# A two-layer transformer block in fp32: the moving tiles of 256 columns read in another order, and the split weights placed 64 bytes later

## The chip, the cores and the metric

One Trainium2 chip, one core of it. The metric is the device time of one execution in microseconds (us), the median of 3 runs. Smaller is better.

## What is computed

The input is one sequence of 256 tokens with 2048 features each, in fp32. The first layer normalises it, multiplies it with a wide input matrix, runs a latent attention of 16 heads and a gated convolution of width 3 side by side, projects both, mixes them with gates and projects once more. The second layer puts 16 meta tokens ahead of the 256, so that it works on 272, and again runs two branches: an attention over the 64 keys that an indexer selects, and a gated recurrence. What takes the time is the same everywhere, products with weights that are read once:

```python
h = _rmsnorm(x, pre_norm_g)
proj = jnp.einsum('bsd,de->bse', h, w_in)            # 2048 x 15424
...
q = jnp.einsum('bsr,re->bse', _rmsnorm(q_a, q_a_norm_g), w_q_b)
kv = jnp.einsum('bsr,re->bse', _rmsnorm(c_kv, kv_a_norm_g), w_kv_b)
y_mla = jnp.einsum('bse,ed->bsd', attn, w_o_mla)
y_conv = jnp.einsum('bse,ed->bsd', b_gate * conv * jax.nn.silu(z_conv), w_o_conv)
out = jnp.einsum('bsd,de->bse', merged, w_out)
...
proj = h @ w_in                                       # second layer, 2048 x 12368
p = jnp.einsum('btnc,ncd->btnd', y, w_branch)
x + merged @ w_out
```

## The kernel before

**Products in three terms.** A weight tile w and an operand tile x are each split into two fp32r numbers, w = w_hi + w_lo and x = x_hi + x_lo, and a product is the sum of three matmuls: w_hi with x_hi, w_hi with x_lo, w_lo with x_hi. All three add up in one PSUM bank.

**The tile.** In `tile` (line 1293 on) the weight, 128 rows by 128 columns, is the stationary operand, and the activation, stored with its 2048 features along 16 tiles of 128 partitions and its 256 tokens along the columns, is the moving one. So one matmul reads 128 stationary columns and 256 moving columns and writes 256 columns of a bank. Kinds that begin with "f" are of this form. Their moving operand has 256 columns (the constant `S`) in most phases; where the second layer needs the meta tokens too (operand `h2_all`) it has 272 (`T`). Kinds that begin with "t" have the roles turned: the activation is stationary and the weights move, 512 columns in the last phase (`wout2`) and two pieces of 128 in the value tiles of phase `kv`. Every matmul has a weight load of its own.

**The work list.** `plan_work` writes the whole program as a list of steps. The weights come in units of 1024 columns (512 KB): SP's queue loads a unit into one of 4 slots of `w_raw`, ACT rounds it into one of 3 slots of `w_hi` (line 1619), DVE subtracts to fill the same slot of `w_lo` (line 1927), and 24 matmuls of TensorE consume it. Units run two to three ahead of TensorE. Everything else (norms, rope, softmax, gates, the recurrence) is put between the units by `pump`.

**Where things lie.** `Memory.__init__` allocates tensors in SBUF one behind another. Per partition `w_raw` takes 16,384 bytes, `w_hi` and `w_lo` 12,288 bytes each. Behind them comes `hb`, which holds the operand tiles of the first layer as rows of 256 columns (1024 bytes), with 16 columns (`ODD`, 64 bytes) ahead of them and 16 behind. `ob_hi` and `ob_lo` hold rows of 272 + 16 columns (1152 bytes); where only the 256 tokens are wanted, the row is read from column 16 on. Counted in lines of 64 bytes from the start of `w_raw`, all split weight tiles begin on even lines, all moving tiles of 256 columns on odd lines, and the moving tiles of 272 columns on even lines.

Of the kernel before, what the change touches and what calls it, by code (L numbers as in the profile page):

```python
# [9 lines left out]
F32R = mybir.dt.float32r  # L10
# [6 lines left out]
P = 128  # L17
D = 2048
KT = D // P
S = 256  # L20
# [97 lines left out]
class Stream:  # L118
# [3 lines left out]
    def __init__(self, eng, own):  # L122
        self.eng, self.own, self.count, self.seen = eng, own, 0, {}
# [85 lines left out]
COLS = lambda m: slice(m * P, (m + 1) * P)  # L209
# [832 lines left out]
ODD = 16  # L1042
MAGIC = 1.5 * 2.0 ** 23
N_LVL = len(LEVELS) * P // 2
L0 = CONSTS["late"][0]

pair = lambda x: x.rearrange("p (h x) -> p h x", h=2)
four = lambda x: x.rearrange("p (a b) -> p a b", a=4)


class Memory:


    def __init__(self, nc, ctx, a):
        def sb(name, shape, dt=F32):
            return ctx.enter_context(nc.sbuf_tensor(name, shape, dt))

        self.raw = sb("w_raw", [P, N_RAW, UNIT])
        self.whi = sb("w_hi", [P, N_SPLIT, UNIT], F32R)
        self.wlo = sb("w_lo", [P, N_SPLIT, UNIT], F32R)  # L1060
        hb = sb("hb", [P, ODD + 2 * KT * S + ODD], F32R)[:, ODD:ODD + 2 * KT * S].rearrange("p (k n) -> p k n", k=2 * KT)
        self.hb_hi, self.hb_lo = hb[:, 0:KT, :], hb[:, KT:2 * KT, :]
        self.ob_hi, self.ob_lo = (sb(n, [P, KT, T + ODD], F32R)[:, :, 0:T] for n in ("ob_hi", "ob_lo"))
        self.arena = sb("arena", [P, 72 * 256])
        self.con = sb("con", [P, CONSTS["resident"][1]])
        self.cols = sb("cols", [P, P])
        self.rope1 = sb("rope1", [P, 2, S])
        self.fac = sb("factor", [P, 3, T])
        self.small = sb("small", [P, 256])
        self.scratch = [sb(f"scratch{i}", [P, T])[:, :] for i in range(5)]  # L1070
        self.heads = [sb(f"head_factor{i}", [P, T])[:, :] for i in range(3)]
        self.acc_a, self.acc_b = sb("acc_a", [P, S])[:, :], sb("acc_b", [P, S])[:, :]
        psum = [ctx.enter_context(nc.psum_tensor(f"bank{i}", [P, 512], F32))[:, :] for i in range(8)]
        self.proj, self.side = psum[:5], psum[5:]
        self.stats = [sb(f"stats{i}", [P, 8])[:, :] for i in range(6)]
        self.prob = [sb(f"prob{i}", [P, 416])[:, :] for i in range(2)]
        self.prob_t = [sb(f"probT{i}", [P, 384])[:, :] for i in range(2)]
        self.small2, small3 = sb("small2", [P, 64]), sb("small3", [P, 2 * HI])
        self.q_factor = sb("q_factor", [P, 2 * HA])
        self.best = sb("best", [P, 16])  # L1080

        r = self.region
        self.Q1, self.QR, self.K1 = r(0, 16, H1, S), r(16, 8, H1 // 2, S), r(24, 16, H1, S)
        self.V1, self.G1 = r(40, 16, 2, D), r(56, 16, KT, S)
        self.LAT = self.V1[:, 0, :].rearrange("p (k n) -> p k n", k=8)
        self.OUT1, self.GM, self.XR = r(40, 16, KT, S), self.K1, r(24, 16, KT, S)
        self.x_in, self.x_meta, self.xT = r(0, 16, 2, D), r(16, 8, D), self.G1
        self.rows_in, self.pos_i = r(24, 1, P), r(25, 1, S)[0:1, :].bitcast(I32)
        self.u_t, self.gate_t = r(56, 4, 4, S), r(60, 4, 4, S)
        self.kr1 = r(68, 1, S)  # L1090
        self.KR2, self.KI2 = r(64, 2, 2, S), r(48, 2.25, 2, T)
        self.pos_f, self.metaT = self.small[0:1, 0:S], self.small[:, :]
        self.metaf = self.metaT.rearrange("p (k n) -> p k n", k=KT)
        s2 = self.small2
        self.lb, self.oml, self.lbx, self.mx = s2[:, 0:8], s2[:, 8:16], s2[:, 16:32], s2[:, 32:40]
        self.acc_m, self.rkv_col, self.q_gain = s2[:, 40:56], s2[:, 56:58], s2[:, 58:59]
        self.wiT = small3[:, :]
        self.R, self.RR, self.RQ = self.fac[:, 0, 0:S], self.fac[:, 1, 0:S], self.fac[:, 2, 0:S]
        self.F2 = self.fac[:, 1, :]
        self.F2M = self.F2[:, NMETA:T]  # L1100

        self.QI, self.KI = r(0, 8, 8, S), r(8, 2, T)
        self.KA, self.QA, self.VA = r(9.25, 4.25, KVA, T), r(13.5, 8, HA, S), r(21.5, 6, 3, 512)
        self.FB, self.IB, self.QB = r(27.5, 8.5, HB, T), r(36, 12, 3, 1024), r(48, 8, HB, S)
        self.GA, self.GB = r(56, 16, KT, S), r(29, 16, KT, S)
        self.late = r(58, 6, CONSTS["late"][1] - L0)
        self.bias2, self.score2 = r(65, 2, 416), r(67, 2, 416)
        self.lvl, self.lvl_in = self.small[:, 0:N_LVL // 4].bitcast(U8), r(69, 2, N_LVL)
        self.prob_m = [self.rope1[:, i, :] for i in range(2)]
        self.Cb, self.Rb, self.kL, self.qL = r(0, 2, W2), r(2, 2, W2), r(4, 2, W2), r(6, 2, W2)  # L1110
        self.A, self.kK, self.kd, self.St, self.kM = r(8, 2, W2), r(10, 2, W2), r(12, 1, S), r(21.5, 2, W2), r(23.5, 4, 1024)
        self.xT2, self.OT = r(29, 16, KT, S), r(0, 16, 2, D)

        self.x_dram = nc.dram_tensor("x_kept", [P, KT * S], F32, kind="Internal").ap()
        self.x1_dram = nc.dram_tensor("x1_kept", [P, KT * S], F32, kind="Internal").ap()
        self.weights = {n: a[n] for n in ("w_in", "w_q_b", "w_kv_b", "w_o_conv", "w_o_mla", "w_out")}
        self.weights |= {"w_in_2": a["w_in_2"][0], "w_branch_a": a["w_branch_2"][0, 0],
                         "w_branch_b": a["w_branch_2"][0, 1], "w_out_2": a["w_out_2"][0]}
# [157 lines left out]
def tensor_engine(nc, m, plan, S_):  # L1276
# [6 lines left out]
    def mm(dst, lhsT, rhs, start=True, stop=True):  # L1283
        return nc.tensor.matmul(dst, lhsT, rhs, start=start, stop=stop, skip_group_check=True)  # L1284

    def operand_ready(name, k):
        if name in ("h2", "h2_all"):
            pe.wait_ge(*done["meta"])
            pe.wait_ge(*done["h2", k])
        elif name in ("lat_q", "lat_kv", "oc", "zm", "mg", "ya", "yb", "mg2", "h"):  # L1290
            pe.wait_ge(*done[name, k])

    def tile(s):
        i, t = s.args
        u, slot = plan.units[i], i % N_SPLIT
        hi_w = m.whi[:, slot, 0:u.size].rearrange("p (k n) -> p k n", k=u.nk)
        lo_w = m.wlo[:, slot, 0:u.size].rearrange("p (k n) -> p k n", k=u.nk)
        if t == 0:
            pe.wait_ge(*plan.split[i]["w_lo"])
        if u.k0 == 0:  # L1300
            pe.wait_ge(*s.of["bank"].after)
        dst = m.out_of(u, t, s.of["bank"].slot)
        kind, j = u.tiles[t][0], int(u.tiles[t][1])
        for k in range(u.nk):
            kt = u.k0 + k
            operand_ready(u.phase.operand, kt)
            x_hi, x_lo = m.operand(u.phase.operand, kt)
            first, last = kt == 0 and not (len(u.tiles) > 4 and t % 2), kt == u.phase.ktiles - 1
            if kind == "f":
                inst = mm(dst, hi_w[:, k, COLS(j)], x_hi, first, False)  # L1310
                inst = mm(dst, hi_w[:, k, COLS(j)], x_lo, False, False)
                inst = mm(dst, lo_w[:, k, COLS(j)], x_hi, False, last)
            else:
                w_hi, w_lo, to = hi_w[:, k, :], lo_w[:, k, :], dst
                if u.phase.name == "kv":
                    w_hi, w_lo, to = heads_kv(w_hi), heads_kv(w_lo), pair(dst)
                inst = mm(to, x_hi[:, COLS(j)], w_hi, first, False)
                inst = mm(to, x_lo[:, COLS(j)], w_hi, False, False)
                inst = mm(to, x_hi[:, COLS(j)], w_lo, False, last)
        if u.last:  # L1320
            inst.then_inc(S_("proj"), 1)
        elif t == len(u.tiles) - 1:
            inst.then_inc(S_("used"), 1)
# [261 lines left out]
    def x1_turn(s):  # L1585
# [5 lines left out]
        turn(b[:, P:S], m.xT2[:, k, P:S], ident).then_inc(S_("x1_t"), 1)  # L1591

    does = dict(tile=tile, constants=constants, warm=warm, pre_cols=pre_cols, x_tile=x_tile, row_sum=row_sum, row_spread=row_spread,
                cols=cols, angle=angle, meta_turn=meta_turn, rope=rope, scores1=scores1, turn1=turn1, mix1=mix1,
                ki_turn=ki_turn, qa_sum=qa_sum, tok_turn=tok_turn, index=index, scores2=scores2, turn2=turn2,
# [1017 lines left out]
```

## Time and profile before

| | |
|---|---|
| median of 3 runs | 1958.9 us (1958.53 to 1958.91) |
| the profiled execution, its own time | 1948.82 us |
| its span (first to last instruction) | 1947.5 us |
| TensorE matmul (PE) busy | 1933.1 us, 99%, 15806 matmuls |
| TensorE weight load (PEld) busy | 1899.4 us, 98%, 15806 loads |
| DVE / ACT / POOL busy | 60% / 45% / 16% |
| DMA | 343.79 MB, mean 177 GB/s |
| granted TensorE clock, mean | 0.998 of full |

The profile names an instruction by engine, line, operation, and "out<-in" by tensor names; `bank<-hb,w_hi` is a matmul that writes a PSUM bank, with `hb` as moving and `w_hi` as stationary operand. Matmuls overlap each other in the records: one is listed with about 280 ns though the next begins far sooner, so the busy time of PE tells nothing of its speed. What tells it is the distance from one start to the next. The timeline gives the starts (neighbours of the same kind are merged there, with xN behind them), and the view by stretches gives how many matmuls lie in a stretch.

### The profile page before, as it was taken

What the parts mean: (1) busy time and instruction counts of PE and PEld (TensorE: products, weight loads), DVE (VectorE), ACT (ScalarE), POOL (GpSimd) and SP (SyncE); (2) the same over time, 40 slices, a digit from 0 to 9 for tenths busy, and PEclk for the clock granted to TensorE, in tenths of its full rate; (3) what the DMA queues carried; (4) which work ended last, traced back from release to release, by engine and by line L of the source; (5) the groups of instructions that cost most, each with busy time, mean ns of one, the idle gap of its engine ahead of it and who ended that gap; (6) DMA issues with size and microseconds to landing.
All of it is one profiled execution on the core that took longest, in us unless ns stands there. A gap on an engine that the chain in (4) does not pass through costs nothing.

```text
span 1947.5 us, 37136 instructions
## 1 busy us (share of the span) xinstructions
PE 1933.1 (99%) x15806; PEld 1899.4 (98%) x15806; DVE 1174.3 (60%) x1708; ACT 880.8 (45%) x1265; POOL 314.9 (16%) x320
## 2 busy tenths in 40 slices
PE   8999999999999999999999999999999999999999
PEld 8999999999999999999999999999999999999987
DVE  7765665556555455654664665676467776654644
ACT  6444454544444434444445543445443333444443
POOL 3210010202010002300122252040011132110200
PEclk9999999999999999999999999999999999999999
DMA  7565555566666566566565564544564444666564
GB/s 262 155 193 173 164 150 152 166 181 184 186 187 198 189 190 179 183 197 195 192 228 189 179 217 130 143 140 122 161 184 142 133 140 142 174 200 188 185 231 157
DMA packets 175919, 343.79 MB, mean 177 GB/s; under 512 B 10494, under 2 KB 19578, under 8 KB 175226
## 3 DMA queue, kind: packets, MB, share of 16 engines
q1 hardware_dynamic: 174106, 337.16, 57.3%
q10 hardware_dynamic: 1648, 4.26, 0.6%
q8 instruction: 124, 2.03, 0.4%
q14 instruction: 41, 0.34, 0.0%
HBM read 335.09 MB, written 6.29 MB: 175 GB/s over the span
## 4 chain that ended last, share of the span: by engine, by line
PE 94%; DVE 1%; issue 0%; POOL 0%; ACT 0%; POOLq 0%; ACTq 0%; DVEq 0%
PE bank L1284 93%; DVE w_lo L1927 1%; DVE hb L2163 0%; ACT w_hi L1619 0%; DVE scratch L2033 0%; DVE ob_lo L2138 0%; POOL scratch L2523 0%; PE bank L1501 0%; PE bank L1590 0%; PE bank L1440 0%; PE bank L1441 0%; PE bank L1439 0%; PE bank L1591 0%; PE bank L1503 0%; POOL acc_a L2452 0%
## 5 line engine op out<-in xcount | busy, mean ns | idle before, releaser
L1927 DVE TENSOR_TENSOR w_lo<-w_raw,w_hi 128x1024 fp32r<-128x1024 f32 (+2 forms) x644 | 785.9, 1224 | 484.8 <-ACT w_hi L1619 483.3
L1619 ACT ACTIVATE w_hi<-w_raw 128x1024 fp32r<-128x1024 f32 (+2 forms) x644 | 662.9, 1032 | 891.7 <-PE bank L1284 882.9
L1284 PE MATMUL bank<-hb,w_hi 128*128 128x256 f32 x4896 | 865.1, 280 | 1.7 <-DVE hb L1951 1.4
L1284 PEld LDWEIGHTS bank<-hb,w_hi 128*128 128x128 f32 x4896 | 745.9, 188 | 5.0 <-DVE w_lo L1927 3.5
L1284 PE MATMUL bank<-hb,w_lo 128*128 128x256 f32 x2448 | 681.7, 278 | 0.0
L1284 PE MATMUL bank<-ob_hi,w_hi 128*128 128x256 f32 (+1 forms) x2224 | 640.4, 288 | 0.1
L1284 PE MATMUL bank<-ob_lo,w_hi 128*128 128x256 f32 (+1 forms) x2224 | 624.8, 281 | 0.0
L1284 PE MATMUL bank<-ob_hi,w_lo 128*128 128x256 f32 (+1 forms) x2224 | 624.2, 281 | 0.0
L1284 PEld LDWEIGHTS bank<-hb,w_lo 128*128 128x128 f32 x2448 | 459.8, 188 | 0.0
L1284 PEld LDWEIGHTS bank<-ob_hi,w_hi 128*128 128x128 f32 x2224 | 418.1, 188 | 2.5 <-DVE w_lo L1927 0.5
L1284 PEld LDWEIGHTS bank<-ob_lo,w_hi 128*128 128x128 f32 x2224 | 418.1, 188 | 1.6
L1284 PEld LDWEIGHTS bank<-ob_hi,w_lo 128*128 128x128 f32 x2224 | 417.4, 188 | 0.0
L1284 PE MATMUL bank<-arena 128*128 128x64 f32 (+4 forms) x618 | 101.7, 302 | 2.6 <-ACT arena L1844 1.6
L1284 PEld LDWEIGHTS bank<-arena 128*128 128x128 f32 x618 | 80.9, 191 | 4.9 <-ACT arena L1844 2.3
L2533 POOL TENSOR_TENSOR arena<-scratch,arena 128x256 f32<-128x256 f32 x32 | 38.4, 1230 | 266.6 <-DVE scratch L2033 266.6
L2033 DVE TENSOR_TENSOR scratch<-bank,factor 128x256 f32<-128x256 f32 (+1 forms) x132 | 52.7, 421 | 36.4 <-PE bank L1284 36.3
L1284 PE MATMUL bank<-w_hi,ob_hi 128*128 128x512 f32 (+1 forms) x192 | 68.9, 359 | 0.0
L1284 PE MATMUL bank<-w_lo,ob_hi 128*128 128x512 f32 (+1 forms) x192 | 68.4, 356 | 0.0
L1284 PE MATMUL bank<-w_hi,ob_lo 128*128 128x512 f32 (+1 forms) x192 | 68.1, 354 | 0.0
L2506 POOL TENSOR_TENSOR arena<-arena,factor 128x256 f32<-128x256 f32 x16 | 19.2, 1233 | 269.3 <-DVE arena L2033 269.3
L2523 POOL TENSOR_TENSOR scratch<-scratch,head_factor 128x256 f32<-128x256 f32 x16 | 12.6, 787 | 236.1 <-ACT head_factor L1737 236.1
L2033 DVE TENSOR_TENSOR arena<-bank,factor 128x256 f32<-128x256 f32 (+1 forms) x86 | 34.4, 419 | 23.6 <-PE bank L1284 23.6
(241 smaller groups left out, 1171.4 us busy)
## 6 DMA issues: line engine op xcount, KB each, us to landing
w_raw<-in_w_in SPq DMA_DIRECT2D x436, 512.0 KB, 3.7
w_raw<-in_w_out SPq DMA_DIRECT2D x64, 512.0 KB, 4.4
w_raw<-in_w_o_conv SPq DMA_DIRECT2D x32, 512.0 KB, 4.1
w_raw<-in_w_o_mla SPq DMA_DIRECT2D x32, 512.0 KB, 4.0
w_raw<-in_w_branch SPq DMA_DIRECT2D x32, 512.0 KB, 4.1
w_raw<-in_w_kv_b SPq DMA_DIRECT2D x16, 512.0 KB, 3.7
w_raw<-in_w_q_b SPq DMA_DIRECT2D x16, 384.0 KB, 3.3
arena<-x_kept SPq DMA_DIRECT2D x2, 2048.0 KB, 9.4
```

The costliest lines, as they stand in the source:

```text
L1284: return nc.tensor.matmul(dst, lhsT, rhs, start=start, stop=stop, skip_group_check=True)
L1619: act(dst, src, ACT.Copy).then_inc(S_("w_hi"), 1)
L1927: tt(low, src, high.bitcast(F32), ALU.subtract).then_inc(S_("w_lo"), 1)
L2033: tt(dst, m.proj[s.of["pb"]][:, 0:dst.shape[1]], factor, ALU.mult).then_inc(S_("evac"), 1)
L2506: tt(m.u_t[:, t, :], m.u_t[:, t, :], m.R, ALU.mult).then_inc(S_("conv_b"), 1)
L2523: tt(z, z, ring[s.of["head"].slot][:, 0:S], ALU.mult).then_inc(S_("silu"), 1)
L2533: tt(y, m.scratch[s.of["scratch"].slot][:, 0:S], y, ALU.add).then_inc(S_("merged"), 1)
```

## The change

It changes two things and nothing else. The number of instructions on each engine and their order stay as they are.

1. Each "f" matmul whose moving tile has 256 columns reads it, and writes its 256 output columns, in another order: in runs of 16 columns (64 bytes), taking run 0, then 8, then 1, then 9, and so on to 7 and 15. Every column still gets the same sum at the same place. Moving tiles of 272 and 512 columns and the value tiles of `kv` keep their order.
2. A tensor of 16 columns (64 bytes) that nothing uses is allocated between `w_raw` and `w_hi`, and the 16 columns ahead of the operand tiles in `hb` go away. So `w_hi` and `w_lo` begin 64 bytes later, and all that comes behind keeps its place. Counted as above, all split weight tiles now begin on odd lines.

```diff
+twos = lambda x: x.rearrange("p (b a e) -> p a b e", b=2, e=16) if x.shape[1] == S else x
...
         self.raw = sb("w_raw", [P, N_RAW, UNIT])
+        sb("odd", [P, ODD])
         self.whi = sb("w_hi", [P, N_SPLIT, UNIT], F32R)
         self.wlo = sb("w_lo", [P, N_SPLIT, UNIT], F32R)
-        hb = sb("hb", [P, ODD + 2 * KT * S + ODD], F32R)[:, ODD:ODD + 2 * KT * S].rearrange("p (k n) -> p k n", k=2 * KT)
+        hb = sb("hb", [P, 2 * KT * S + ODD], F32R)[:, 0:2 * KT * S].rearrange("p (k n) -> p k n", k=2 * KT)
...
             if kind == "f":
-                inst = mm(dst, hi_w[:, k, COLS(j)], x_hi, first, False)
-                inst = mm(dst, hi_w[:, k, COLS(j)], x_lo, False, False)
-                inst = mm(dst, lo_w[:, k, COLS(j)], x_hi, False, last)
+                x_hi, x_lo, to = twos(x_hi), twos(x_lo), twos(dst)
+                inst = mm(to, hi_w[:, k, COLS(j)], x_hi, first, False)
+                inst = mm(to, hi_w[:, k, COLS(j)], x_lo, False, False)
+                inst = mm(to, lo_w[:, k, COLS(j)], x_hi, False, last)
```

## Rows read from the trace of the kernel before

**Rows 1.** The page: the span, and the chain that ended last by engine.
```profile
span 1947.5 us, 37136 instructions
...
PE 94%; DVE 1%; issue 0%; POOL 0%; ACT 0%; POOLq 0%; ACTq 0%; DVEq 0%
```

**Rows 2.** Groups of PE by form: count, busy us, mean ns | idle before.
```profile
L1284 PE MATMUL bank<-hb,w_hi 128*128 128x256 f32 x4896 | 865.1, 280 | 1.7 <-DVE hb L1951 1.4 <-DVE w_lo L1927 0.2
L1284 PE MATMUL bank<-hb,w_lo 128*128 128x256 f32 x2448 | 681.7, 278 | 0.0
L1284 PE MATMUL bank<-ob_hi,w_hi 128*128 128x256 f32 x1824 | 518.7, 284 | 0.1
...
L1284 PE MATMUL bank<-ob_hi,w_hi 128*128 128x272 f32 x400 | 121.6, 304 | 0.0
```

**Rows 3.** PE by stretches: from:to, us, busy (matmuls), granted clock, DMA share, GB/s.
```profile
410.00:560.00 150.00, 149.99 (x1274) 1.00 0.63 183
580.00:640.00 60.00, 60.00 (x532) 1.00 0.66 194
660.00:730.00 70.00, 70.00 (x602) 1.00 0.59 188
750.00:830.00 80.00, 79.97 (x676) 1.00 0.60 181
850.00:910.00 60.00, 60.00 (x532) 1.00 0.67 200
930.00:1000.00 70.00, 70.00 (x602) 1.00 0.58 189
```

**Rows 4.** PE timeline near 500 us: start us, listed us, instruction, how many.
```profile
500.13 0.40 PE L1284 MATMUL bank<-hb,w_hi 128*128 128x256 f32 x2
...
501.19 0.28 PE L1284 MATMUL bank<-hb,w_hi 128*128 128x256 f32 x1
```

**Rows 5.** PE timeline near 600 us.
```profile
600.02 0.39 PE L1284 MATMUL bank<-hb,w_hi 128*128 128x256 f32 x2
...
600.70 0.28 PE L1284 MATMUL bank<-hb,w_hi 128*128 128x256 f32 x1
```

**Rows 6.** PEld timeline near 500 us: the weight loads beside rows 4.
```profile
500.02 0.31 PEld L1284 LDWEIGHTS bank<-hb,w_hi 128*128 128x128 f32 x2
500.25 0.19 PEld L1284 LDWEIGHTS bank<-hb,w_lo 128*128 128x128 f32 x1
```

**Rows 7.** PE timeline near 1862 us: last phase, and four transposes in it.
```profile
1862.17 0.39 PE L1284 MATMUL bank<-w_hi,ob_hi 128*128 128x512 f32 x1
...
1865.18 0.39 PE L1284 MATMUL bank<-w_hi,ob_lo 128*128 128x512 f32 x1
...
1865.65 0.27 PE L1590 MATMUL bank<-con,arena 128*128 128x128 f32 x1
...
1865.98 0.27 PE L1591 MATMUL bank<-con,arena 128*128 128x128 f32 x1
```

**Rows 8.** PE timeline near 1160 us: moving tiles of 272 columns.
```profile
1159.98 0.29 PE L1284 MATMUL bank<-ob_hi,w_hi 128*128 128x272 f32 x1
...
1161.11 0.29 PE L1284 MATMUL bank<-ob_hi,w_hi 128*128 128x272 f32 x1
```

**Rows 9.** PE timeline near 140 us: value tiles of phase kv, moving in two pieces.
```profile
140.52 0.28 PE L1284 MATMUL bank<-w_hi,ob_hi 128*128 128x256 f32 x1
...
141.10 0.28 PE L1284 MATMUL bank<-w_lo,ob_hi 128*128 128x256 f32 x1
```

**Rows 10.** Waits: who waited for whom: us in total, times, longest.
```profile
PEld bank L1284 <- DVE w_lo L1927: 4.1, 11, 1.6
...
ACT w_hi L1619 <- PE bank L1284: 882.9, 527, 3.6
```

**Rows 11.** The page: the split of a unit on DVE, and the load of one.
```profile
L1927 DVE TENSOR_TENSOR w_lo<-w_raw,w_hi 128x1024 fp32r<-128x1024 f32 (+2 forms) x644 | 785.9, 1224 | 484.8 <-ACT w_hi L1619 483.3
...
w_raw<-in_w_in SPq DMA_DIRECT2D x436, 512.0 KB, 3.7
```

## The prediction

> **What bounds the kernel now.** First the chain of waits, summed by engine: TensorE holds 94% of the span [rows 1], and of its weight loads' waits the longest sum is 4.1 us, for `w_lo` [rows 10]. ACT, on the other hand, waited 882.9 us for TensorE to give weight slots back [rows 10]. So the work that feeds TensorE has room, and the time is the number of matmuls times the distance between two starts. The groups by form give the numbers: with a moving tile of 256 columns there are 4896 + 2448 from `hb`, and 1824 in each of three groups from `ob`, 12,816 in all; the tiles of 272 columns are 3 x 400 [rows 2].
>
> Then the distance, the number on which all hangs. By stretches: six stretches hold 490 us and 4218 matmuls; a matmul is listed for 0.28 us, so each stretch also counts some 2.4 that began before it, and 490 us over 4204 is **116.6 ns** [rows 3]. It isn't one pace: 1274 in 150 us is 118.0 ns and 532 in 60 us is 113.3 ns [rows 3]. The timelines say the same: from 500.13 to 501.19 lie nine starts, 117.8 ns each [rows 4], from 600.02 to 600.70 six, 113.3 ns each [rows 5]. The instructions, the tensors (`hb`, `w_hi`, `w_lo`) and the granted clock (1.00, the level of 2.4 GHz) are alike. At that clock 256 columns, one in each cycle, are 106.7 ns. So 7 to 11 ns of each matmul are lost to something that depends on how two things fall together in time, not on what is computed.
>
> What falls together? The next weight load begins within 10 ns behind each matmul's start (500.25, beside the second of the two that are merged from 500.13 on) [rows 4, 6]. Stationary and moving columns are read from the same memory side by side. And what a pair can't go below is seen in the transposes of the last phase, 128 moving columns and a weight load each: three distances in 0.33 us, 110 ns [rows 7], though 128 columns in one pass are 53 ns. I take **110 ns** as the floor of a load and matmul pair.
>
> **The change, part by part.**
>
> *The order of the columns.* It adds and removes no instruction. In the order before, moving lines of 64 bytes alternate between odd and even every 16 columns, 6.7 ns; the stationary lines alternate every 13.8 ns (110 ns over 8 lines). If memory has two sides, chosen by odd and even lines, then the two streams must meet on one side for half the time, wherever they begin. In the new order two lines of the same side follow each other, 0 and 8, then 1 and 9, so both streams change sides every 13 to 14 ns: once they are apart they stay apart. That such sides exist no row shows directly; what speaks for it is that the loss grows with the moving columns and isn't a fixed cost per matmul: 272 columns take 125.6 ns (nine distances in 1.13 us) against 113.3 at the clock [rows 8], 512 columns take 231.5 ns (13 in 3.01 us) against 213.3 [rows 7]; and that two paces exist at all. The cost is bounded from both sides. Below: the floor of 110, or 106.7 if the weight load could go faster than in transposes; above: load and read strictly one after the other, 110 + 107 = 217 ns. The old order, which meets half the time, pays only 6.6 ns over the floor, so I take the value near the lower end: 116.6 - 110 = 6.6 ns, times 12,816: **-85 us**.
>
> A rule speaks against this. The Trainium skill (SBUF — State Buffer, "Who interferes with whom") says that TensorE has two independent read ports, one for the moving operand and one for the weights, and never waits on anyone; by that rule the sum of this part would be 0. Rows 4 and 5, two paces of the same instructions, are hard to square with it, but they don't name the memory as the cause.
>
> *Reading and writing in runs.* A read in pieces is seen once: the value tiles of `kv` move two pieces of 128 columns and take 116 ns (five distances in 0.58 us) [rows 9], no more than their neighbours. For runs of 16 and for output in runs there is no row; I put them at 0 (the read row is the nearest), with the rival below as the upper end.
>
> *The weights 64 bytes later.* ACT and DVE write them at another address, in operations of the same length (DVE 1224 ns a unit [rows 11], against 24 x 116.6 = 2800 ns that TensorE needs for it). What changes is with which line both streams begin: before, stationary even and moving odd; now both odd. Whether that is the right side can't be read from the trace, since the two reads' true offset isn't in it. In my forecast it costs 0; the wrong side is a rival. For the tiles of 272 columns the order stays and only this shift acts: at most the difference of the two paces, 4.5 ns, up or down, times 1200, +-5 us; I take 0.
>
> *What is late next.* At 110 ns a unit lasts 24 x 110 = 2640 ns. The load of a unit lands in 3.7 us with up to four in flight, and the DMA share of 0.57 to 0.67 [rows 3] becomes at most 0.67 x 117/110 = 0.71. DVE's split still fits, but other DVE work stands in the same queue, so some more waits for `w_lo` come: I double the 4.1 us [rows 10], **+4 us**.
>
> Sum: -85 + 4 = **-81 us**. Against the profiled execution, 1948.8 us, that is 1868; the median of the runs is 1958.9, 10 us above it, and the same difference gives **1878 us**.
>
> **The rivals.**
>
> 1. *Only the better of the two present paces.* The streams settle at 113.3 ns everywhere, as in rows 5. For it: that pace is held for 60 us on end twice [rows 3], so it is a stable state. Against it: it arises with the old order. (116.6 - 113.3) x 12,816 = 42 us: 1917 us.
> 2. *Nothing changes* (the change does not do what its order suggests). The loss is inside TensorE or on the way of each column, and order and place of the lines don't matter. For it: the loss per column is nearly the same for 256, 272 and 512 columns, though in the last case the weight load ought to be over after half the time. 1959 us, within the +-5 us of the other tiles.
> 3. *Slower: both streams begin on the same side.* The new order keeps two moving lines on one side, so a wrong start costs a whole stationary line, 13.8 ns, before they are apart, and every matmul with its own weight load begins anew: 110 + 13.8 = 123.8 ns, 7.2 ns more than now, times 12,816: +92 us, 2051 us. It decides from the point where more than 6.6 ns of each start are lost, half a line. For it: both operands now begin on odd lines and within 10 ns of each other [rows 6]. Against it: the loads' data may be wanted a line earlier or later than the starts say, in which case the shift is just what sets them apart. A smaller loss is as possible as a whole line.
> 4. *Slower: the output in runs.* 16 runs a matmul instead of one; if each of the 15 jumps costs one cycle, 0.42 ns, the gain of 6.6 ns is used up (6.3), and with two cycles each matmul takes 110 + 12.5 = 122.5 ns: +76 us, 2035 us. No row has such an output. The Trainium skill (PSUM — Partial Sum Buffer, "Specifications") says that PSUM has lines of 8 bytes and any non-contiguous pattern slows matmuls significantly. By that rule this is the case; no run here shows it, and within a run of 16 columns everything is contiguous, so I hold it less likely.
>
> **How the numbers follow.** Forecast 0.48, rival 1 0.17, rival 2 0.09, rival 3 0.16, rival 4 0.10. Differences under 0.2% (4 us) can't be told from no change here. Faster by more: 0.48 + 0.17 = 0.65. Within: 0.09. Slower: 0.26. The forecast's own range is 1850 (108 ns a pair, as the floor is read from rows rounded to 10 ns) to 1905. The range for 8 in 10 begins at 1850 and takes in rivals 1 and 2 and the milder half of 3 and 4, where a third to half of the priced loss is paid: up to 2000. The case of 217 ns, 1.3 ms more, is left out, as is most of a full extra line.
>
> **What would show it.** In the changed kernel the stretches of rows 3 should hold about 545 matmuls in 60 us instead of 532 or 510, all at one pace, and the timeline six starts in 0.66 us. Rival 1: 0.68 us everywhere; rival 2: two paces as now; rivals 3 and 4: 0.72 us and more. Rival 4 would slow the tiles of 256 columns by the same in every stretch, while rival 3 could differ between them. The 272 column tiles should stay near 125 ns, DVE's split at 1224 ns. I am wrong if the pace stays above 115 ns, or if it falls and the time doesn't follow, which would show as waits for `w_lo`.

## The result, and the profile after

The changed kernel takes **1995.9 us** (median of 4 runs, 1992.7 to 1996.9) against 1958.7 for the kernel before, measured beside it (4 runs, 1957.9 to 1958.9): ratio 1.020, 95% interval 1.018 to 1.022. I had forecast 1878. The profiled execution took 1995.2 us, 46.4 us more than that of before. It lies inside my range of 1850 to 2000, but on the other side of no change, so that the range holds it is luck.

First the page and the groups by form of the changed kernel, in the form of [rows 1, 2]:

```profile
span 1993.9 us, 37136 instructions
...
PE 97%; DVE 1%; DMA 1%; issue 1%; ACT 0%; POOL 0%; SPq 0%; POOLq 0%; ACTq 0%
...
L1286 PE MATMUL bank<-hb,w_hi 128*128 128x256 f32 x4896 | 890.6, 284 | 0.6 <-DVE hb L1954 0.5
...
L1286 PE MATMUL bank<-ob_hi,w_hi 128*128 128x256 f32 x1824 | 527.6, 289 | 0.0
```

The chain has grown even more into one of matmuls, 97% where it was 94%, and the counts are the same. So the time is again the number of matmuls times the distance between two starts. The same stretches as in [rows 3] (from:to, us, busy and matmuls, granted clock, DMA share, GB/s):

```profile
410.00:560.00 150.00, 150.00 (x1250) 1.00 0.62 182
580.00:640.00 60.00, 60.00 (x502) 1.00 0.63 183
660.00:730.00 70.00, 70.00 (x581) 1.00 0.56 181
750.00:830.00 80.00, 80.00 (x668) 1.00 0.61 177
850.00:910.00 60.00, 60.00 (x502) 1.00 0.65 188
930.00:1000.00 70.00, 70.00 (x580) 1.00 0.56 183
```

The counts add up to 4083 instead of 4218. Less the 2.4 of each stretch that began before it, that is 490 us over 4069 matmuls, **120.4 ns** instead of 116.6. The difference of 3.8 ns times the 12,816 tiles of 256 columns is 49 us; the span grew by 46.4. So the whole loss is in the distance of the starts, at the same granted clock of 1.00, and the 2.6 us left over are less than what the readings carry. The timeline shows something that the mean doesn't. Start, listed time, instruction, how many; near 500 us and near 600 us, beside [rows 4, 5]:

```profile
500.15 0.40 PE L1286 MATMUL bank<-hb,w_hi 128*128 128x256 f32 x2
...
501.23 0.40 PE L1286 MATMUL bank<-hb,w_hi 128*128 128x256 f32 x2
```

```profile
599.93 0.40 PE L1286 MATMUL bank<-hb,w_hi 128*128 128x256 f32 x2
...
600.65 0.40 PE L1286 MATMUL bank<-hb,w_hi 128*128 128x256 f32 x2
```

Nine starts in 1.08 us and six in 0.72 us: 120.0 ns in both places. Before it was 117.8 and 113.3. The two paces have become one, slower than either. Over the whole trace the mean distance with a moving tile from `hb` is 120.0 ns (before 116.4), and with one from `ob` 121.0 (before 116.9).

What feeds TensorE is not involved. Here are the waits of the weight loads and of ACT (who for whom: us in total, times, longest), DVE's split and the landing of a unit:

```profile
PEld bank L1286 <- DVE w_lo L1930: 1.1, 2, 0.7
...
ACT w_hi L1622 <- PE bank L1286: 938.6, 539, 3.6
```

```profile
L1930 DVE TENSOR_TENSOR w_lo<-w_raw,w_hi 128x1024 fp32r<-128x1024 f32 (+2 forms) x644 | 785.1, 1222 | 514.2 <-ACT w_hi L1622 512.2
...
w_raw<-in_w_in SPq DMA_DIRECT2D x436, 512.0 KB, 3.7
```

The weight loads waited 1.1 us for `w_lo` instead of 4.1, and ACT 938.6 us for TensorE instead of 882.9 [rows 10]; a unit is split in 1222 ns and lands in 3.7 us, as in [rows 11]. The tiles of 272 columns, which the new order leaves alone, take 125 ns (six starts, 0.75 us), as in [rows 8]:

```profile
1190.84 0.29 PE L1286 MATMUL bank<-ob_hi,w_lo 128*128 128x272 f32 x1
...
1191.59 0.29 PE L1286 MATMUL bank<-ob_hi,w_lo 128*128 128x272 f32 x1
```

### The profile page after: what moved, and what is told of

It reads as the page before. It is cut to its first block, busy times and chain, and to the rows that moved or that the text cites. A ratio compares the mean times of both kernels' runs of the same rounds, so it can differ in the third digit from the quotient of the medians.

```text
span 1993.9 us, 37136 instructions
## 1 busy us (share of the span) xinstructions
PE 1980.4 (99%) x15806; PEld 1948.3 (98%) x15806; DVE 1175.0 (59%) x1708; ACT 879.9 (44%) x1265; POOL 315.1 (16%) x320
## 4 chain that ended last, share of the span: by engine, by line
PE 97%; DVE 1%; DMA 1%; issue 1%; ACT 0%; POOL 0%; SPq 0%; POOLq 0%; ACTq 0%
PE bank L1286 96%; DMA w_raw<-in_w_in 1%; DVE w_lo L1930 0%; ACT w_hi L1622 0%; POOL scratch L2526 0%; PE bank L1504 0%; DVE arena L1949 0%; ACT scratch L1641 0%; PE bank L1442 0%; PE bank L1444 0%; PE bank L1594 0%; PE bank L1593 0%; PE bank L1443 0%; PE bank L1506 0%; POOL acc_a L2455 0%
## 5 line engine op out<-in xcount | busy, mean ns | idle before, releaser
L1930 DVE TENSOR_TENSOR w_lo<-w_raw,w_hi 128x1024 fp32r<-128x1024 f32 (+2 forms) x644 | 785.1, 1222 | 514.2 <-ACT w_hi L1622 512.2
L1622 ACT ACTIVATE w_hi<-w_raw 128x1024 fp32r<-128x1024 f32 (+2 forms) x644 | 662.6, 1032 | 942.8 <-PE bank L1286 938.6
L1286 PE MATMUL bank<-hb,w_hi 128*128 128x256 f32 x4896 | 890.6, 284 | 0.6 <-DVE hb L1954 0.5
L1286 PEld LDWEIGHTS bank<-hb,w_hi 128*128 128x128 f32 x4896 | 761.8, 191 | 2.7 <-DVE w_lo L1930 1.1
L1286 PE MATMUL bank<-hb,w_lo 128*128 128x256 f32 x2448 | 692.9, 283 | 0.0
L1286 PE MATMUL bank<-ob_hi,w_hi 128*128 128x256 f32 (+1 forms) x2224 | 648.7, 292 | 0.0
L1286 PE MATMUL bank<-ob_lo,w_hi 128*128 128x256 f32 (+1 forms) x2224 | 635.1, 286 | 0.0
L1286 PE MATMUL bank<-ob_hi,w_lo 128*128 128x256 f32 (+1 forms) x2224 | 633.9, 285 | 0.0
L1286 PEld LDWEIGHTS bank<-hb,w_lo 128*128 128x128 f32 x2448 | 467.1, 191 | 0.0
L1286 PEld LDWEIGHTS bank<-ob_hi,w_lo 128*128 128x128 f32 x2224 | 422.3, 190 | 0.0
L2536 POOL TENSOR_TENSOR arena<-scratch,arena 128x256 f32<-128x256 f32 x32 | 38.4, 1222 | 278.6 <-DVE scratch L2036 278.6
```

What stands on the lines that cost most here:

```text
L1622: act(dst, src, ACT.Copy).then_inc(S_("w_hi"), 1)
L1930: tt(low, src, high.bitcast(F32), ALU.subtract).then_inc(S_("w_lo"), 1)
L2536: tt(y, m.scratch[s.of["scratch"].slot][:, 0:S], y, ALU.add).then_inc(S_("merged"), 1)
```

## The experiments

Paces are distances of starts, means over one kind of tile in a whole trace; "hb" is the moving tile of 256 columns from `hb`, "ob" that from `ob_hi` or `ob_lo`. Distances of 150 ns and more, which are waits or other work in between, are left out. Where no interval is given a kernel ran once; the kernel before took 1952 to 1962 us in the runs beside these. Line numbers move a little from kernel to kernel. Diffs are against the kernel before.

### The two parts of the change, each alone

The order alone leaves all addresses as they were:

```diff
+                x_hi, x_lo, to = twos(x_hi), twos(x_lo), twos(dst)
+                inst = mm(to, hi_w[:, k, COLS(j)], x_hi, first, False)
...
```

> The new column order with the addresses of before (stationary even, moving odd). Theory A (the new order keeps the two streams in step but the 64-byte shift put them on the same side at the start): the distance of two starts falls below 113 ns, towards 110, and the time below 1920 us. Theory B (output in runs is slow in itself): about 120 ns as in the changed kernel, 1990 to 2000 us. Theory C (the sides exist, but the offset of the two reads is somewhere between): another value between 113 and 124 ns.

The shift alone is the second part of the diff of the change, with every tile read in its natural order:

```diff
+        sb("odd", [P, ODD])
         self.whi = sb("w_hi", [P, N_SPLIT, UNIT], F32R)
...
-        hb = sb("hb", [P, ODD + 2 * KT * S + ODD], F32R)[:, ODD:ODD + 2 * KT * S].rearrange("p (k n) -> p k n", k=2 * KT)
+        hb = sb("hb", [P, 2 * KT * S + ODD], F32R)[:, 0:2 * KT * S].rearrange("p (k n) -> p k n", k=2 * KT)
```

> Split weights 64 bytes later, natural order. Theory A: natural order meets on one side half of the time wherever it begins, so 113 to 118 ns as before and 1950 to 1970 us. Theory B: the same. Theory D (the shift alone is what costs): about 120 ns, near 1995 us.

Measured: the order alone 1998.5 us, 1.022 times the kernel before (1.020 to 1.024); the shift alone 1982.6 us, 1.014 (1.012 to 1.016). Stretches of the two, the order first:

```profile
580.00:640.00 60.00, 60.00 (x503) 1.00 0.58 180
660.00:730.00 70.00, 70.00 (x577) 1.00 0.55 181
```

```profile
580.00:640.00 60.00, 60.00 (x503) 1.00 0.58 180
660.00:730.00 70.00, 70.00 (x591) 1.00 0.56 186
```

In the `hb` phases (first row) either part alone brings the full loss: 120.0 ns with the order, 119.9 with the shift, 120.0 with both. In the `ob` phases (second row) the order costs more than the shift: 121.4 and 118.7 ns. The two do not add. My forecast took the shift for a mere choice of the side on which the new order begins, and that has fallen: the order costs as much at the old addresses as at the new. With that rival 3 is out as the cause of the order's loss: the order alone puts the starts back on different lines, as before, and gets nothing back. What is left of rival 3 is its condition: with the shift alone, both operands begin on odd lines, and that does cost.

### Read or write

Only the output in runs, or only the moving operand in runs (the columns of the output are then in another order than the reference's):

```diff
+                to = twos(dst)
+                inst = mm(to, hi_w[:, k, COLS(j)], x_hi, first, False)
...
```

> Addresses of before; the moving tile is read in natural order, only the 256 output columns are written in the order of runs, so that the output columns are permuted (values are not the reference's). Theory B (output in runs is slow): 120 ns and over 1985 us. Theory A: paces of before, 113 to 118 ns, about 1959 us.

```diff
+                x_hi, x_lo, to = twos(x_hi), twos(x_lo), dst
+                inst = mm(to, hi_w[:, k, COLS(j)], x_hi, first, False)
...
```

> Addresses of before; the moving tile is read in runs 0, 8, 1, 9, the output written in natural order, so that the output columns are permuted (values are not the reference's). Theory A: like the kernel with both in runs (below 113 ns). Theory B: not slow, 110 to 117 ns. If reading in runs costs in itself: 120 ns.

Measured: writing 1952.5 us with 116.6 and 117.1 ns, reading 1998.1 us with 120.0 and 121.4 ns. The same two stretches, the write first and then the read:

```profile
410.00:560.00 150.00, 149.99 (x1274) 1.00 0.59 184
...
850.00:910.00 60.00, 60.00 (x531) 1.00 0.62 194
```

```profile
410.00:560.00 150.00, 150.00 (x1250) 1.00 0.58 183
...
850.00:910.00 60.00, 60.00 (x502) 1.00 0.60 189
```

Writing in runs keeps the counts of before in these stretches, 1274 and 531 or 532 [rows 3], and has 512 instead of 532 from 580 to 640 us, where this execution held the slower of the two old paces; reading in runs has the counts of the changed kernel. The loss of the order lies in the read of the moving operand, and rival 4 has fallen. The Trainium skill (PSUM — Partial Sum Buffer, "Specifications") says that any non-contiguous pattern in PSUM slows matmuls significantly; sixteen runs of 64 bytes cost nothing here (116.6 ns against 116.4), so in this form the measurement decides against it.

### Are there two sides, by 64-byte lines?

If the sides existed, a moving stream that reads one line sixteen times and a stationary stream that reads one column 128 times could be held on opposite sides for good. Each of these kernels computes something else than the reference: all columns of a tile come from its first 16 columns, or all rows of a weight tile from its first column.

```diff
+one = lambda x: x[:, 0:16].unsqueeze(1).to_broadcast([P, 16, 16]) if x.shape[1] == S else x
+still = lambda w: w[:, 0:1].to_broadcast([P, P])
...
```

> Addresses of before. Each moving tile of 256 columns reads its first 16 columns, one odd line of 64 bytes, sixteen times (values are not the reference's). Theory A2 (the loss comes from both reads being on the same side): the stationary read is on the other side for half of its lines, so some loss stays, 112 to 118 ns, or the two settle apart and it is near 110. Theory F (the loss is in the moving read's own steps from line to line, whatever the stationary read does): no steps, no loss, 109 to 110 ns, about 1865 us. If one side for all 16 reads is worse than changing sides: over 118 ns.

> Addresses of before, moving tiles as in the kernel before; each weight load of these matmuls reads one column 128 times, so one even line (values are not the reference's). Theory A2: paces differ from before, either way. Theory F: 113 to 118 ns as before, about 1955 us.

> Both at once: moving reads one odd line, stationary one even line (values are not the reference's). Theory A2: always on different sides, so this is the floor, 109 to 110 ns and about 1865 us. Theory F: the same 109 to 110 ns, as with the moving read alone. If it is 113 ns or more, the loss isn't in the lines read at all.

And an order that keeps to one side for the first half of a tile and to the other for the second, lines 0, 2, 4 to 14, then 1, 3 to 15:

```diff
+twos = lambda x: x.rearrange("p (a b e) -> p b a e", b=2, e=16) if x.shape[1] == S else x
```

> Addresses of before, runs of 16 columns taken 0, 2, 4 up to 14, then 1, 3 up to 15, for read and write: eight lines of one side, then eight of the other. Theory A2: the stationary read alternates, so it meets the moving read on half of its lines: 113 to 120 ns. Theory F (only steps cost, jumps more than neighbours): about 120 ns as with the order 0, 8, 1, 9.

| kernel | us | hb ns | ob ns |
|---|---|---|---|
| one line, moving | 2011.2 | 122.2 | 120.9 |
| one column, stationary | 1933.1 | 114.2 | 116.7 |
| both | 2013.4 | 122.2 | 121.9 |
| even lines first | 1996.5 | 120.1 | 121.1 |

The kernel before took 1958.6 us beside these. A stretch with one column stationary, and the same stretch with both:

```profile
850.00:910.00 60.00, 60.00 (x531) 1.00 0.62 194
```

```profile
850.00:910.00 60.00, 60.00 (x493) 1.00 0.58 182
```

The pair that by my theory can never meet is the slowest of all, 493 matmuls in 60 us. Theory F of the expectations, that each step of the moving read to another line costs, wanted 109 to 110 ns for it and for one line moving, and missed as well. This pair has a weakness as a test, since a read of the same 16 columns may have a price of its own (the probes below say that it has). The even lines first have no such weakness: with them the two streams meet half the time, as in the natural order, so the theory as the prediction used it wants 116.6 ns (the expectation left it up to 120), and they cost what the order of the change costs, 120.1. The next probes settle it: the order of the change takes 120.0 ns with the weights on either side. So the theory on which 0.48 of the chances and -85 us rested is refuted as an account of the order, not only in its sign.

That the stationary read has some part in the pace is seen with one column stationary. The mean of 114.2 ns in `hb` against 116.4 shows less than it seems to, since most of it is how many groups of output columns hold the better pace: steady groups run at 113.33 or 116.67 ns, in the kernel before at 113.33 or 117.78. But the slower of the two is 1.1 ns shorter, and the tiles of 272 columns, for which this kernel loads one column too, take 124.3 ns instead of 125.8.

### Probes of many variants in one kernel

To see more than one value in a run, the next kernels choose a variant for every group of output columns. The slots of `w_hi` and `w_lo` grow by 128 columns so that a weight tile can begin `at` columns later, and `w_raw` loses a slot to make room; the order of the reads is chosen in the same table.

```diff
+VARIANTS = [(at, same, same, same) for at in (0, 4, 8, 12, 16, 20, 24, 32, 48, 64, 96, 112)]
...
+def slot_of(w, u, slot):
+    at = variant(u)[0]
+    return w[:, slot, at:at + u.size]
...
+                _, read, write, still = variant(u) if u.phase.n == S else (0, same, same, same)
+                to = write(dst)
+                inst = mm(to, still(hi_w[:, k, COLS(j)]), read(x_hi), first, False)
...
```

> A probe for paces, not for its total: three slots of w_raw instead of four, weight slots of 1152 columns, and each group of 512 output columns (or 384, 1024) puts its split weights 0, 4, 8, 12, 16, 20, 24, 32, 48, 64, 96 or 112 columns behind the slot's start, in turn. Natural order of the moving columns. Theory G (what counts is the distance of the two streams by lines of 64 bytes, with two sides): 0, 32, 64, 96 alike at 113 to 118 ns and 16, 48, 112 alike at 120 ns in the hb phases. If more address bits count, 32 or 64 differ from 0. If smaller units count, 4, 8 and 12 lie apart from 0 and 16.

> A probe for paces: three slots of w_raw, and each group reads and writes the 256 columns in one of eight orders (natural; halves interleaved in runs of 16, 32, 64 and 8 columns; quarters in runs of 16; even lines first in runs of 16 and 32), each with the split weights at 0 and 16 columns. Theory H (a jump in the moving read costs, whatever the lines are): the loss grows with the number of runs, so 8 column runs over 120 ns, 16 columns 120, 32 columns about 118, 64 columns as natural. Theory G (what counts is how sides follow one another): runs of 16 with halves interleaved and even lines first differ from each other, the number of runs doesn't order them.

> A probe for paces: three slots of w_raw, and each group reads natural, one line sixteen times (line 0, 1 or 3), 8 columns 32 times, 32 columns 8 times, 64 columns 4 times, 128 columns twice, or one column 256 times, each with the split weights at 0 and 16 columns; the last variant also loads one column as all 128 stationary ones (values are not the reference's). Theory H: loss grows with the number of jumps; one column without any jump in its pattern is at 110 ns. Theory G: 32 columns 8 times, which alternates between two sides as natural does, is like natural; one line sixteen times is 122 ns whichever line it is, and one column 256 times too.

Paces here are means behind the first 24 matmuls of a group, over the two to four groups of a variant; the times of the whole kernels (1968.8, 1992.8 and 1974.6 us, beside 1952.2 for the kernel before) mix all variants and say little.

Place of the weights, natural order, `hb` ns: at 0 columns 117.5, at 4 117.4, at 8 117.0, at 12 118.9, **at 16 119.9**, at 20 118.3, at 24 118.3, at 32 116.4, at 48 118.8, at 64 117.2, at 96 114.7, at 112 118.7. Single groups at 0, 32, 64 and 96 run at 117.8 or, at 32 and 96, at 113.4, and some between the two; 16 gives 119.9, and 48 and 112 give 118.7 or 118.8. At 12 the groups lie from 117.3 to 120.0. So the place matters with a period of about 32 columns, 128 bytes, though not exactly. In addresses: at 0 the moving and the weight tile begin 64 bytes apart, counted modulo 128 bytes (odd and even lines); at 16 they begin at the same place modulo 128.

Order of the moving columns, halves interleaved as in the change, weights at 0 and at 16 columns, `hb` ns:

| length of a run | at 0 | at 16 |
|---|---|---|
| natural | 117.5 | 120.0 |
| 64 columns | 117.3 | 119.9 |
| 32 columns | 118.8 | 119.0 |
| 16 columns (the change) | 120.0 | 120.0 |
| 8 columns | 123.3 | 123.3 |

With runs of 16 the weights' place has no effect, 120.0 at both, where by the theory of sides one of them had to be good. The even runs of 16 first, another interleaving, is again 120.0 at both places. The length of a run counts, but it isn't all. The same runs of 16 with quarters interleaved (0, 4, 8, 12, then 1, 5 and so on) take 118.8 ns as a mean at both places (at 16 columns its two groups take 120.0 and 117.6), and runs of 32 with the even ones first take 120.1 and 118.7, by groups from 117.3 to 120.2. Two stretches of 18 us, halves in runs of 16 first, then quarters in runs of 16:

```profile
578.00:596.00 18.00, 18.00 (x152) 1.00 0.63 198
...
854.00:872.00 18.00, 18.00 (x154) 1.00 0.62 199
```

Less the 2.4 these are 120.3 and 118.7 ns. So how the runs follow each other counts too, by up to 1.3 ns. Repeated reads set the other end: the first 16 columns sixteen times 121.9 and 122.8 (two other lines of 16 columns 120.1 to 123.0), 32 columns eight times 120.0 and 118.4, 64 columns four times 117.8 and 120.0, but 8 columns 32 times **111.67** at either place, and so does one column 256 times:

```profile
870.04 0.39 PE L1309 MATMUL bank<-hb,w_hi 128*128 128x256 f32 x2
...
870.71 0.39 PE L1309 MATMUL bank<-hb,w_hi 128*128 128x256 f32 x2
```

Six starts in 0.67 us, 111.7 ns each, and the weights' place has no effect. This is the fastest that a pair with 256 moving columns ran here, and so the floor as far as these runs go, not the 110 ns that I had taken from transposes of 128 columns [rows 7].

### What is it in the read?

Two theories were left. J: columns are fetched in pieces of 32 bytes (8 columns), and a run costs by the pieces it touches. H: each jump in the pattern costs, so that the loss grows with the number of runs.

```diff
+from_to = lambda at, n: lambda x: x[:, at:at + n].unsqueeze(1).to_broadcast([P, S // n, n])
+READS = [(same, same), (from_to(0, 8), split(8)), (from_to(4, 8), split(8)), (from_to(8, 8), split(8)), (from_to(0, 4), split(4)),
+         (from_to(8, 16), split(16)), (runs(2, 8), runs(2, 8)), (runs(2, 4), runs(2, 4)), (runs(2, 2), runs(2, 2))]
```

> A probe for paces, three slots of w_raw. The groups read in turn: natural; 8 columns 32 times beginning at column 0, 4 or 8; 4 columns 64 times; 16 columns 16 times beginning at column 8; halves interleaved in runs of 8, 4 and 2 columns (those three correct, the repeated ones not); each with the split weights at 0 and 16 columns. Theory J (the loss is paid when the moving read comes to another piece of 8 columns, 32 bytes): 8 columns from 0 or 8 at 111.7 ns, the same 8 columns begun at column 4, which touch two pieces, 120 ns or more; 4 columns 64 times 111.7; runs of 4 and 2 columns above the 123.3 ns of runs of 8, as pieces change 64 and 128 times instead of 32. Theory H (jumps in the pattern cost): 8 columns 32 times would not be at the floor, and the start column would make no difference.

Eight columns repeated from column 4 on lie in two pieces of 32 bytes, and take 111.67 ns like those from column 0 or 8. J has fallen. So has H as it stands in the expectation, which wanted the repeated 8 columns off the floor, 31 jumps back being jumps too. Shorter runs of the interleaved halves cost more: 8 columns 123.3 ns, 4 columns 126.7 (weights at 0) and 128.9 (at 16), 2 columns about 170. The timeline of the runs of 4, nine starts in 1.14 us, 126.7 ns, and of the runs of 2, nine starts in 1.48 us, 164 ns here:

```profile
1100.97 0.41 PE L1308 MATMUL bank<-hb,w_hi 128*128 128x256 f32 x2
...
1102.11 0.29 PE L1308 MATMUL bank<-hb,w_hi 128*128 128x256 f32 x1
...
1696.13 0.50 PE L1308 MATMUL bank<-hb,w_hi 128*128 128x256 f32 x2
...
1697.61 0.50 PE L1308 MATMUL bank<-hb,w_hi 128*128 128x256 f32 x2
```

What is left of H is a description, put together after these results: with halves interleaved the loss grows with the number of runs that come from a new place, and what repeats within 8 columns costs nothing. The quarters and the even runs of 32 above don't fit it. What in the read takes the time remains open. (The whole kernels of this probe and the next took 2023.6 and 1972.6 us, beside 1960.1 for the kernel before.)

For the shift the question was another: does the address of the weights count, or only its distance from that of the moving tile (theory K)? Here the moving tile too is read `back` columns earlier (so its columns are other ones than the reference's):

```diff
+VARIANTS = [(at, back, same, same) for back in (0, 4, 8, 12, 16) for at in (0, 8, 16, 24)]
...
+            return (self.hb_flat[:, ODD + (k + i) * S - back:ODD + (k + i) * S - back + S] for i in (0, KT))
```

> A probe for paces, three slots of w_raw, natural order. The moving tiles are read 0, 4, 8, 12 or 16 columns before their true start (values are not the reference's; not in the first tile of a sum, and not for the tiles from ob in the first layer), each with the split weights at 0, 8, 16 and 24 columns. Theory K (only the distance between the two places counts): moving 16 back with weights at 0 equals moving 0 back with weights at 16, 120 ns, and moving 16 back with weights at 16 equals the place of before, 113 to 118 ns. Theory J adds: 4 or 12 back, where the tile touches 33 pieces instead of 32, is a little slower than 0 or 8 back. If both places count for themselves, neither holds.

`hb` ns, by how much earlier the moving tile and how much later the weights begin, in columns:

| moving earlier by | weights at 0 | at 8 | at 16 | at 24 |
|---|---|---|---|---|
| 0 | 115.7 | 116.8 | 119.9 | 118.4 |
| 8 | 116.7 | 119.9 | 118.3 | 113.4 |
| 16 | 119.9 | 118.3 | 113.4 | 117.3 |

The rows are the same series, each one place further: in these steps of 8 columns what counts is the sum, the distance, and it begins anew at 32 columns (115.7 is a mean of groups at 113.4 and at 117.7). The two rows left out fit less well: 4 columns earlier 118.4, 116.8, 117.2 and 117.5 ns, 12 columns earlier 118.6, 117.1, 118.7 and 119.2, so that a distance of 28 is once 117.5 and once 118.7. Between the steps K holds only roughly. The timelines of three fields with the distance 16: at 529 us (16 and 0) and 911 us (8 and 8), nine starts in 1.08 us, 120.0 ns; and with the distance 32, at 574 us (16 and 16), six starts in 0.68 us, 113.3 ns:

```profile
528.92 0.40 PE L1311 MATMUL bank<-hb,w_hi 128*128 128x256 f32 x2
...
530.00 0.28 PE L1311 MATMUL bank<-hb,w_hi 128*128 128x256 f32 x1
...
574.03 0.39 PE L1311 MATMUL bank<-hb,w_hi 128*128 128x256 f32 x2
...
574.71 0.39 PE L1311 MATMUL bank<-hb,w_hi 128*128 128x256 f32 x2
...
910.73 0.40 PE L1311 MATMUL bank<-hb,w_hi 128*128 128x256 f32 x2
...
911.81 0.40 PE L1311 MATMUL bank<-hb,w_hi 128*128 128x256 f32 x2
```

### Whole kernels for the two findings

K says that the weights' shift costs nothing if the moving tiles are shifted along, H that runs of 64 cost nothing and runs of 8 about twice as much as those of 16. The first only allocates the 64 unused bytes and keeps those in `hb`, so that all comes 64 bytes later; the others change a number of the order of the change, at the old addresses:

```diff
+        sb("odd", [P, ODD])
         self.whi = sb("w_hi", [P, N_SPLIT, UNIT], F32R)
```

> Natural order; the unused 64 bytes stand ahead of w_hi and nothing is taken away, so split weights, hb and ob all lie 64 bytes later and keep their distances. Theory K (only the distance counts): as before, 1950 to 1960 us. If the place of w_hi itself counts: near 1983 us as in shift_only. If the two groups of the probe that ran at 113.4 ns in this arrangement tell of a steadier good pace: down to 1925 us.

```diff
+twos = lambda x: x.rearrange("p (b a e) -> p a b e", b=2, e=64) if x.shape[1] == S else x
```

> Addresses of before, halves interleaved in runs of 64 columns, four runs. Theory H (the loss grows with the number of runs): near the kernel before, 1950 to 1962 us, 117 ns.

> Addresses of before, halves interleaved in runs of 8 columns, 32 runs. Theory H: 123.3 ns as in the probe, 12816 times 6.7 ns over the kernel before, so 2030 to 2045 us.

Measured: all later 1960.6 us, 1.0007 times the kernel before (0.999 to 1.002); runs of 64 1959.3 us; runs of 8 2029.5 us, with 123.3 ns in `hb` and 123.1 in `ob`. The first stretches of all later and one of the runs of 8:

```profile
410.00:560.00 150.00, 149.98 (x1274) 1.00 0.63 183
580.00:640.00 60.00, 60.00 (x511) 1.00 0.64 189
```

```profile
580.00:640.00 60.00, 60.00 (x489) 1.00 0.63 180
```

Both findings hold in whole kernels. (With all later the distance stays what it was; a distance of 32 columns, at which all four groups of the last probe ran at 113.4 ns, was not tried in a whole kernel.) The 511 where [rows 3] have 532 is the natural order's other pace: 117.8 ns in this execution where it was 113.3 in that one. The kernel before ranged from 1948.8 us in its profiled execution to 1962. The share of the two paces is the likely reason, though no slower execution of it has a trace: by its paces (116.4 and 116.9 ns against 117.5 and 117.2 in all later) its profiled execution should be 7344 x 1.1 + 5472 x 0.3 = 10 us shorter, and its span is, 1947.5 against 1959.1 us, 12 us.

## Why the prediction was wrong

**What bounds the kernel** was right. Matmuls times distance accounts for the result as well (49 us against 46.4), and no feeding wait took part.

**The order of the columns, -85 us: this step failed.** It built on memory with two sides chosen by odd and even lines of 64 bytes, which no row showed; I had said so and still gave it 0.48. The runs put +3.6 ns in `hb` and +4.5 ns in `ob` in place of -6.6 (the order alone, 120.0 and 121.4 against 116.4 and 116.9), 7344 x 3.6 + 5472 x 4.5 = +51 us, and the span of the order alone is 1997.7 - 1947.5 = 50 us longer than that of before. The order costs the same with the weights at either place, and two streams held on opposite lines are no faster. The signs that I read as support, a loss that grows with the columns and two paces of the same instructions, are real, but at most they told that two things meet in time, not by what address.

**The rule of independent ports.** After the row on the two paces I cited the Trainium skill (SBUF — State Buffer, "Who interferes with whom") for a sum of 0. That rule came out no better: the distance between the two operands' addresses alone moves the pace from 113.4 to 119.9 ns. Which resource they share no run shows.

**Reading and writing in runs, 0.** Half right. Writing is free (116.6 ns). The nearest row for reading had two pieces of 128 columns [rows 9], too far from sixteen of 16: pieces of 64 cost nothing either, those of 16 cost the full 3.6 ns. This 0 is the second step that failed: the read in runs alone brings the loss of the whole change.

**The weights 64 bytes later, 0.** Wrong as a cost, by the shift alone 7344 x 3.6 + 5472 x 1.8 = +36 us, and its span is 1983.4 - 1947.5 = 36 us longer. In the changed kernel the shift adds nothing to this in `hb`, where either part alone already gives 120 ns. (The profiled execution of before was one of its faster; against the medians beside them the order costs 44 us and the shift, by its ratio, 27.) I had priced the wrong side only as the rival 3 of the new order, and at the natural order not at all. That the tiles of 272 columns would stay within 5 us was right: 125.1 ns against 125.8 over the trace, 1 us less. For them the shift goes the other way, from the same place modulo 128 bytes to 64 bytes apart, and it helps.

**What is late next, +4 us**, had no occasion, since no unit got shorter; the waits for `w_lo` fell from 4.1 to 1.1 us.

**The floor.** The fastest pace seen with 256 columns is 111.67 ns, not 110. Even a change that removed all loss above it could give only (116.6 - 111.7) x 12,816 = 63 us, not 85. Rival 1 was priced too high as well: both stretches at 113.3 ns are `hb` phases. The `ob` phases never held that pace; the better of their two is 116.67 ns ([rows 3] have 602 matmuls in 70 us there). The better pace everywhere would be worth 7344 x 3.0 + 5472 x 0.2 = 23 us, not 42.

**The rivals.** The sign was that of rivals 3 and 4, their "0.72 us for six starts" is what the timeline shows, and 1995.9 us lies in the milder half that the range took in; that was luck, because neither mechanism is the cause. Rival 3 fell with the order alone and with the one-line pair, rival 4 with the write alone. A rival was missing: that the read in runs itself has a price. I had priced jumps in the output at one or two cycles each, but no jumps in the input, though for both the trace had no row with more than two pieces.

## What to carry to other kernels

A moving operand of fp32r matmuls with a weight load each and 256 columns was read best in one run or in runs of 64 columns; a regrouping of the output in runs of 16 cost nothing, so put it there rather than in the read. Before moving a tensor by some bytes, look at the distance between the moving and the stationary tiles modulo 128 bytes: 64 bytes apart was good here and 0 bad, a shift of both together is free, and 64 bytes of one alone cost 1.4% of this kernel. Where the argument is that two streams meet at certain addresses, the rows must show a pace at a second address before a layout is priced by it.

## What the runs showed of the hardware that was not expected

- **Distance of addresses.** In the `hb` phases the pace of the same matmul is 113.3 or 117.8 ns with the two tiles 64 bytes apart modulo 128, and 119.9 with both at the same place modulo 128, whichever of the two is moved; between them the means are 116.7 to 119. In the `ob` phases the effect is weaker (116.7 and 118.9 in steady stretches).
- **Two stable paces.** At the good distance in `hb` whole groups of output columns run at 113.33 ns and others at 117.78 (in `ob` at 116.67 and 117.78). The same group can hold the one pace in one kernel and the other in another whose distance is the same: from 587 to 652 us it is 113.33 in the kernel before and with runs of 64, 117.78 in all later and with the output in runs. With the 64-byte shift or halves in runs of 16 there is one pace in `hb`, 120.0. Why the natural order has two is open; a kernel that kept the better one everywhere would gain 23 us, and no version here did.
- **Length of a run** in the moving read, halves interleaved: 64 columns 117.3 ns, 32 118.8, 16 120.0, 8 123.3, 4 126.7, 2 about 170. Up to 8 columns repeated come at the floor of 111.67, whether they begin at column 0, 4 or 8, but 16 repeated take 120 to 123. With quarters interleaved runs of 16 take 118.8.
- **Output in runs** of 64 bytes is free, 116.6 ns against 116.4.
- Not tried: other types than fp32r, and moving tiles of 512 columns in runs.
